# Two chained transformer models: the modulation panels on TensorE in four column groups instead of partly on GpSimd

## The chip, the cores and the metric

One core of one Trainium2 chip. The metric is the time of one execution on the device in microseconds (us); the kernel before has a median of 2692.15 us over three runs (2691.78, 2692.15, 2695.29). Less is better. TensorE multiplies, VectorE and ScalarE do elementwise work and read TensorE's results from the eight PSUM banks, GpSimd does elementwise work in SBUF, and SyncE issues the loads of the weights.

## The reference, cut to what matters

Two models in a row, each of two layers, on 256 tokens of width 1024. The first has a mixing part (layer 0: block attention "moba" and a pooling; layer 1: a gated MLP and a gated delta rule), a cross attention and a convolution FFN in each layer. The second is modulated by a vector c:

```python
def adaln(x, g, shift, scale):
    return rmsnorm_2(x, g) * (1 + scale[:, None, :]) + shift[:, None, :]

for l in range(DEPTH):                       # 2 layers
    mod = jax.nn.silu(c) @ ada_w[l] + ada_b[l]          # c is [1, 1024], ada_w[l] is [1024, 6144]
    sh_m, sc_m, g_m, sh_f, sc_f, g_f = jnp.split(mod, 6, axis=-1)
    hn = adaln(x, mix_norm_g[l], sh_m, sc_m)
    ...                                      # hn @ w_in[l]; four attentions; y = concat @ w_out[l]
    x = x + g_m[:, None, :] * y
    hn = adaln(x, ffn_norm_g[l], sh_f, sc_f)
    ...                                      # f = swiglu (layer 0), top-2-of-8 experts (layer 1)
    x = x + g_f[:, None, :] * f
```

One of the four attentions, the indexed one, scores all keys by `relu(q_idx . k_idx)` in eight heads of 32, weights and sums the heads, and keeps the best 64 keys of each query. Another, the differential one, is normalised per head behind the attention.

## The kernel before, in words

All weights reach SBUF as panels of 1 MB (128 partitions x 2048 floats), issued by SyncE in one fixed order into a ring of six slots. `load_one` waits, before it issues panel n, until panel n-6 is released (`released`), so a panel is issued when the product that reads the one six places ahead is done. 48 of the 583 panels hold the modulation weights `ada_w`: 2 layers x 6 parts x 4 quarters of 256 columns, in the order of `ADA_ORDER`. Parts 2 and 5 are the gates (rows, kept in GATE); the others are shift and scale (columns, kept in MODC).

Before the change, the panels go two ways. 17 are multiplied on TensorE by `ada` (L1071): a stationary COND of 128x128 (silu(c), spread over 128 columns), 256 moving columns, eight products for each panel, into the banks from 4 on. `ADA_AT` gives the places: one panel each at xat0, ffn0, mix1, xat1 and ffn1, four at mix2, three at ffn2, three at mix3 and two at ffn3. `transpose_norm` (L623) calls `ada` first and then waits for the normalised rows (`xhat_ready`), so that these products stand in the time in which the norm is computed. VectorE reads them out in `ada` (L2325 to L2334).

The other 31 panels are lent to GpSimd (`lend` L557, `LENT_AHEAD`): `sum_lent` (L2717) multiplies a panel with silu(c) in four pieces (L2731), adds (L2734, L2736) and leaves 128 x 256 partial sums in one of three buffers LENTS (L2737). `take` (L565) joins the partitions on TensorE with a product against ones (L573 for gates, L576 for columns), and VectorE reads that in `taken`. GpSimd holds two panels in the mixing of layer 0, ten in the cross attention xat0, eleven in mix1 and eight in xat1.

The stages follow one another as mix0 (moba), xat0, ffn0, mix1 (with the levels of a triangular inverse and the delta rule), xat1, ffn1, mix2, ffn2, mix3, ffn3 (experts). Each has a norm before it: ScalarE squares and sums the rows of H (L1474), VectorE makes the factor and XH (L1954), TensorE transposes XH (L632), ScalarE and VectorE read the transposes out with gain or modulation. At the entries of the FFNs ScalarE has first to split the first halves of the first gate and up panels into a high and a low part (`first_halves` L1423, the copy is at L1457); then it squares. VectorE does the low part (L2124). In the FFN TensorE's up products are L885, the down products L899.

The moba attention (`paired_attention` L651) goes over eight units in pairs: scores (L677), softmax on ScalarE and VectorE (scaling by the reciprocal: L2008), transposes (L664), mixing with the values (L693, outputs in two column groups of 64). Panels of the next stages are multiplied beside the units (`BESIDE`). The pooling product L1106 and the projection (`project`, L838) follow; each projection reads four panels. In mix2 and mix3 TensorE scores the index heads with `index_scores` (L1285), tile by tile; ScalarE evacuates them (L1873); VectorE sums them (`index_sum`, L2633 and L2635); the panels c_qi, c_ki, b_qd, b_kvd, a_q, a_k, a_v come between. The squares of the differential output, DSQ, are made on ScalarE in `keep` (L1584), amid the attention of the last groups, and summed on TensorE behind it by `diff_sums` (L758).

A name of a bank is claimed by TensorE (`claim`; `claim_aside` takes one of two banks in turn), filled, read out by another engine, and then free again. All engines work through their own stream in order.

## Time and profile before

| | |
|---|---|
| median of three runs | 2692.15 us |
| the profiled execution, its time | 2694.97 us |
| its span (first to last instruction) | 2693.2 us |
| mean granted clock of TensorE | 0.982 |
| busy: TensorE, VectorE, ScalarE, GpSimd | 2578.2 us (96%), 1726.7 (64%), 1306.3 (49%), 301.1 (11%) |
| `ada` on TensorE (L1083) | 272 records, 60.2 us busy |
| GpSimd's products (L2731) | 124, 130.8 us busy |
| panels in SyncE's queue, ada_w | 48, 4.8 us from issue to landing (median) |

The profile is read for what TensorE waits for: it is busy for 96% of the span, and the chain of work that ended last runs almost wholly through it. The busy shares of the other engines are an average over stages that differ much: the experts fill the second half of the span, while the modulation panels all lie in the first 1645 us. A product of floats (f32) stands as two records in the trace. The duration of a group of records ends with a modelled tail, so prices of products are taken from start to start. "granted clock" 1.0 is 2.4 GHz and 0.50 is 1.2 GHz.

### The profile page before, as it was taken

Reading aid. Unit: us, or ns where it says so; the run is one execution under the profiler, and the core shown is the slowest. Engines: PE = TensorE matmul, PEld = TensorE weight load, DVE = VectorE, ACT = ScalarE, POOL = GpSimd, SP = SyncE. Lnnn points to the kernel's source line nnn. Section 1 sums busy time; section 2 is a strip of 40 time slices with the busy share of each in tenths; the row PEclk is TensorE's granted clock in tenths of the full one; section 3 lists DMA queues with packets and bytes.
Section 4 is the critical chain, followed back from the end, with each engine's and each line's share of the span. In section 5 each row is a group of like instructions: output and inputs, shape, how many; then the busy total and the mean of one; then the engine's idle time right before and its main releaser. Section 6 shows DMA issues by size and latency. Waiting matters only on the chain.

```text
span 2693.2 us, 39037 instructions
## 1 busy us (share of the span) xinstructions
PE 2578.2 (96%) x13620; PEld 2139.9 (79%) x13620; DVE 1726.7 (64%) x2535; ACT 1306.3 (49%) x1931; POOL 301.1 (11%) x288
## 2 busy tenths in 40 slices
PE   7899999999899999989999988999999999999998
PEld 7677899887487998767998766888888888887886
DVE  1312777663225773465553464989898988889897
ACT  2211544421123442243331243777777777777775
POOL 0465000870270000000000000000000000000000
PEclk9999999999899999999999998999999999999999
DMA  8345544442355444315444313989898989899897
GB/s 321 125 179 213 208 185 168 177 174 92 110 219 198 190 183 179 110 48 195 183 183 174 107 58 135 377 320 383 325 379 323 370 329 378 335 346 355 341 355 285
DMA packets 87635, 627.29 MB, mean 233 GB/s; under 512 B 9760, under 2 KB 9920, under 8 KB 12800
## 3 DMA queue, kind: packets, MB, share of 16 engines
q1 hardware_dynamic: 84512, 613.45, 60.1%
...
HBM read 625.06 MB, written 1.05 MB: 232 GB/s over the span
## 4 chain that ended last, share of the span: by engine, by line
PE 92%; DVE 4%; ACT 2%; issue 1%; POOL 1%; DMA 0%; DVEq 0%; SPq 0%; ACTq 0%; POOLq 0%
PE bank L994 23%; PE bank L885 14%; PE bank L1022 11%; PE bank L605 11%; PE bank L899 7%; PE bank L618 6%; PE bank L838 6%; PE bank L1122 1%; PE bank L1083 1%; PE bank L964 1%; PE bank L1037 1%; PE bank L1009 1%; PE bank L677 1%; PE bank L693 1%; PE bank L664 1%
## 5 line engine op out<-in xcount | busy, mean ns | idle before, releaser
L1457 ACT ACTIVATE sb_parts<-sb_ring 128x1024 fp32r<-128x1024 f32 x873 | 872.9, 1053 | 125.4 <-PE bank L1022 38.9
L2222 DVE TENSOR_TENSOR sb_parts<-sb_ring,sb_parts 128x1024 fp32r<-128x1024 f32 x675 | 786.4, 1217 | 10.8 <-ACT sb_parts L1457 10.8
L994 PE MATMUL bank<-sb_parts 128*128 128x512 f32 x2688 | 661.4, 396 | 2.5 <-DVE sb_parts L2214 1.8
L994 PEld LDWEIGHTS bank<-sb_parts 128*128 128x128 f32 x2688 | 495.0, 188 | 113.3 <-issue 9.4
L885 PE MATMUL bank<-sb_parts 128*128 128x256 f32 x3168 | 387.1, 284 | 7.1 <-DVE sb_XT L2147 5.8
L885 PEld LDWEIGHTS bank<-sb_parts 128*128 128x128 f32 x3168 | 385.9, 193 | 9.9 <-issue 7.7
L1022 PE MATMUL bank<-sb_parts 128*128 128x512 f32 x1344 | 323.9, 390 | 0.0
L1022 PEld LDWEIGHTS bank<-sb_parts 128*128 128x128 f32 x1344 | 251.7, 188 | 52.1
L1457 ACT ACTIVATE sb_REG<-bank 128x512 f32<-128x512 f32 (+2 forms) x119 | 67.9, 576 | 408.3 <-PE bank L605 211.4
L605 PE MATMUL bank<-sb_XT,sb_ring 128*128 128x256 f32 x1152 | 257.5, 384 | 6.9 <-DVE sb_XT L1969 3.9
L2124 DVE TENSOR_TENSOR sb_parts<-sb_ring,sb_parts 128x1024 fp32r<-128x1024 f32 x198 | 232.8, 1219 | 34.3 <-ACT sb_parts L1457 34.3
L605 PEld LDWEIGHTS bank<-sb_XT,sb_ring 128*128 128x128 f32 x1152 | 219.5, 192 | 40.4 <-issue 10.9
L899 PE MATMUL bank<-sb_parts 128*128 128x512 f32 x792 | 185.3, 390 | 0.0
L838 PE MATMUL bank<-sb_ring,sb_OT 128*128 128x512 f32 x384 | 169.8, 603 | 3.3 <-DVE sb_OT L2033 1.7
L899 PEld LDWEIGHTS bank<-sb_parts 128*128 128x128 f32 x792 | 146.6, 188 | 29.4 <-DVE sb_parts L2124 0.2
L2731 POOL TENSOR_TENSOR sb_ring<-sb_ring,sb_small 128x512 f32<-128x512 f32 x124 | 130.8, 1085 | 197.5 <-DVE sb_XH L1954 165.4
L838 PEld LDWEIGHTS bank<-sb_ring,sb_OT 128*128 128x128 f32 x384 | 73.6, 193 | 94.6 <-issue 91.5
L618 PE MATMUL bank<-sb_ring,sb_XT 128*128 128x256 f32 (+1 forms) x512 | 117.5, 391 | 5.8 <-ACT sb_O L1873 4.2
L618 PEld LDWEIGHTS bank<-sb_ring,sb_XT 128*128 128x128 f32 x512 | 99.1, 202 | 22.6 <-issue 9.2
L1457 ACT ACTIVATE sb_parts<-bank 128x256 fp32r<-128x256 f32 (+1 forms) x130 | 52.7, 413 | 122.0 <-PE bank L1009 112.2
L1474 ACT ACTIVATE sb_XH<-sb_H 128x1024 f32<-128x1024 f32 x24 | 25.2, 1049 | 161.9 <-DVE sb_H L2097 102.0
L2236 DVE TENSOR_TENSOR sb_parts<-bank,sb_parts 128x256 fp32r<-128x256 f32 x112 | 47.3, 422 | 76.1 <-ACT sb_parts L1457 76.1
...
## 6 DMA issues: line engine op xcount, KB each, us to landing
sb_ring<-in_moe_panels SPq DMA_DIRECT2D x342, 1024.0 KB, 5.0
sb_ring<-in_ada_w SPq DMA_DIRECT2D x48, 1024.0 KB, 4.8
sb_ring<-in_ffn_w_up SPq DMA_DIRECT2D x44, 1024.0 KB, 4.9
sb_ring<-in_ffn_w SPq DMA_DIRECT2D x33, 1024.0 KB, 4.8
sb_ring<-in_w_in SPq DMA_DIRECT2D x26, 1024.0 KB, 4.8
sb_ring<-in_ffn_w_down SPq DMA_DIRECT2D x22, 1024.0 KB, 7.1
sb_ring<-in_xattn_wkv SPq DMA_DIRECT2D x16, 1024.0 KB, 6.9
sb_ring<-in_od_w_in SPq DMA_DIRECT2D x12, 1024.0 KB, 5.6
```

What stands on the lines that cost most here:

```text
L605: m = nc.tensor.matmul(ps[:, c * T:c * T + T], wt[:, k, c * P:c * P + P], rhs[:, k, :], start=k == 0, stop=k == KD - 1)
L618: m = nc.tensor.matmul(ps[:, tb * T:tb * T + w], lhs[:, k, tb * P:tb * P + P], wt[:, k, 0:w], start=k == 0, stop=k == KD - 1)
L838: m = nc.tensor.matmul(acc[j][:, :], OT[:, 2 * pair + c, j // 2 * P:j // 2 * P + P], wt[:, c, j % 2 * 512:j % 2 * 512 + 512], start=kk == ...
L885: m = nc.tensor.matmul(banks[b][:, half * T:half * T + T], w[:, kk, :], x[:, kk, :], start=t == 0, stop=t == len(terms) - 1)
L899: m = nc.tensor.matmul(banks[4 + j][:, :], h[:, g, tb], w[u][:, half], start=start and c == 0 and t == 0, stop=stop and c == 1 and t == 2, ...
L994: m = nc.tensor.matmul(banks[par][:, :], x[:, k, :], w[:, cols], start=k == 0 and t == 0, stop=k == KD - 1 and t == 2, skip_group_check=True)
L1022: m = nc.tensor.matmul(banks[4 + j][:, :], h[:, par, c, :], w[:, cols], start=start and c == 0 and t == 0, stop=stop and c == 1 and t == 2 ...
L1457: return nc.scalar.activation(out, in_, ACT.Copy)
L2124: V_.tensor_tensor(as_panel(LOW[u], what), half_panel(n, what, c, it), as_panel(HIGH[u], what), ALU.subtract).then_inc(sem("low_ready"), 1)
L2222: V_.tensor_tensor(LOW[u], ring[slot][:, 1024 * c:1024 * c + 1024], HIGH[u], ALU.subtract) \
L2236: V_.tensor_tensor(HTL[:, par, :, :], banks[6 + par][:, 0:T].rearrange("p (c t) -> p c t", c=2), HTH[:, par, :, :], ALU.subtract).then_inc ...
L2731: m = G.tensor_tensor(w[:, k:k + 2, :], w[:, k:k + 2, :], c[:, k:k + 2, :], ALU.mult)
```

## The change

- `lend`, `sum_lent`, LENTS, COND, SPREAD and `ADA_AT` go; GpSimd has no part in the modulation.
- The 48 panels form 24 pairs; `ADA_PAIRS` gives two pairs (four panels) to each of twelve places: in moba before the mixing of the last but one pair of units, at xat0, ffn0, mix1, in the levels 2 and 3 of mix1 (one pair each), behind the scan of the delta rule, at xat1, ffn1, mix2, ffn2, mix3, ffn3.
- `ada` takes a stationary operand of 32 columns (silu(c) of one k, broadcast) and puts the product k into the output partitions 32 (k mod 4) and on: eight products for a panel as before, k = 0 to 3 into four column groups and k = 4 to 7 added to them. Two panels share a bank of 512 columns.
- ScalarE copies the bank (128x512) into one of four buffers PARTIAL (`partials`): after the read-out of the norm in most places, in the FFNs before the walk over the chunks.
- `take(i)` joins the pair's partial sums against ones, on TensorE; VectorE scales by 1/32 and adds the bias or the row. The takes of pairs 0 to 3 stand in xat0, 4 to 7 behind the qkv panels of mix1, 8 and 9 in levels 4 and 5, 10 to 13 in xat1, 14 to 17 in mix2, 18 to 21 in mix3, 22 and 23 in the experts. Pairs 4, 5, 10, 11, 16, 17, 22 and 23 are gates.
- `index_scores` claims two banks and emits the products of its two tiles in turn.
- The squares DSQ move from `keep` to behind the whole attention.
- In moba the panel p1 is multiplied beside unit 2 instead of unit 1.

The diff, cut: left out are the old `ada` (L1071, removed), the calls of `index_scores` (now with a pair of tiles), the removed calls of `lend`, the calls of `take` and `taken` that only change their argument, VectorE's `ada` and GpSimd's `sum_lent`, both removed whole.

```diff
@@ -153,9 +153,7 @@
         ROW = sb("ROW", ROW_W)
         REG_W = 13900
         small = sb("small", 544)
-        COND = sb("COND", KD, P)
-        LENTS = sb("LENTS", 3, T)
-        SPREAD = sb("SPREAD", 2, P)
+        PARTIAL = sb("PARTIAL", 4, 2 * T)
         ROUNDS = sb("rounds", 1, dt=mybir.dt.int32)
         small_index = sb("small_index", NT, 8, dt=U32)
         MODC = sb("MODC", 2, 48)
...
@@ -492,26 +490,14 @@
 
 
         ADA_ORDER = [("ada", l, part, q) for l in range(2) for part in range(6) for q in range(4)]
-        ADA_AT = {"xat0": 1, "ffn0": 1, "mix1": 1, "xat1": 1, "ffn1": 1, "mix2": 4,
-                  "ffn2": 3, "mix3": 3, "ffn3": 2}
-
-
-        LENT_AHEAD = {"mix0": (("out", "mix0", 0), ("out", "mix0", 2)),
-                      "xat0": tuple(("xq", 0, j) for j in range(4)) + (("xk", 0, 0), ("xk", 0, 1)) + tuple(("xv", 0, j) for j in range(4)),
-                      "mix1": tuple(("qkv", j) for j in range(6)) + (("u", 0), ("u", 1), ("vz", 0), ("vz", 1), ("gate", 0)),
-                      "xat1": tuple(("xq", 1, j) for j in range(4)) + tuple(("xv", 1, j) for j in range(4))}
-
-
-        TAKE_LATER = {"xat0": {("xq", 1): (2, 4), ("xq", 3): (1, 5), ("xk", 0): (1, 6), ("xk", 1): (1, 7),
-                               0: (1, 7), 1: (1, 6), 2: (1, 7), 3: (1, 6), 4: (1, 7), 5: (1, 6), 6: (1, 7)},
-                      "xat1": {("xq", 2): (1, 4), ("xq", 3): (1, 5), 0: (1, 7), 1: (1, 6), 2: (1, 7), 3: (1, 6),
-                               5: (1, 7), 6: (1, 6)}}
-        LENT_TO = {name: stage for stage, names in LENT_AHEAD.items() for name in names}
-        lent, taken_by = [], {}
+        ADA_PAIRS = {h: (2 * i, 2 * i + 1) for i, h in enumerate(
+            ("moba", "xat0", "ffn0", "mix1", "levels", "delta", "xat1", "ffn1", "mix2", "ffn2", "mix3", "ffn3"))}
+        TAKE_AFTER = {"xat0": {("xq", 1): 0, ("xq", 3): 1, ("xk", 0): 2, ("xk", 1): 3},
+                      "xat1": {("xq", 0): 10, ("xq", 1): 11, ("xq", 2): 12, ("xq", 3): 13}}
         EARLY_KEYS = 4
 
 
-        BESIDE = {"moba": {0: ("p", 0), 1: ("p", 1), 4: ("xk", 0, 2), 6: ("xk", 0, 3)},
+        BESIDE = {"moba": {0: ("p", 0), 2: ("p", 1), 4: ("xk", 0, 2), 6: ("xk", 0, 3)},
                   "x0": {j: ("xv", 0, j) for j in range(4)},
                   "x1": {j: ("xv", 1, j) for j in range(4)}}
         LATE = {0: "d_q", 1: "d_k", 3: "d_v", 4: "c_q", 5: "c_k", 6: "c_v"}
@@ -519,7 +505,7 @@
         SELECT_AT = {0: (0, 0, 4), 1: (0, 4, 8), 3: (1, 0, 4), 4: (1, 4, 8)}
         BIAS_AT = 6
         KEYS_FIRST = {0: (0, 1), 1: ()}
-        ada_done, ada_hooks, ada_panels = [0], {}, {}
+        ada_panels = {}
 
 
         GAINS = {"mem": ("mem_norm", 0), "mix0": ("norm_mix", 0), "mix1": ("norm_mix", 8), "xat0": ("norm_xattn", 0),
...
@@ -554,28 +540,40 @@
                     b, n = turns[name]
                     pe.wait_ge(drained[b], n)
 
-            def lend(stage):
-
-                lent.append((state["panel"], ADA_ORDER[ada_done[0]], stage))
-                ada_panels[state["panel"]] = ADA_ORDER[ada_done[0]]
-                ada_done[0] += 1
-                released[state["panel"]] = (sem("panel_summed"), len(lent))
-                state["panel"] += 1
-
-            def take(hook, n, bank=None):
-
-                first = sum(len(x) for x in taken_by.values())
-                taken_by[hook] = list(range(first, first + n))
-                ps = claim_aside(("taken", hook)) if bank is None else claim(("taken", hook), bank)
-                for x, i in enumerate(taken_by[hook]):
-                    pe.wait_ge(sem("panel_summed"), i + 1)
-                    if lent[i][1][2] in (2, 5):
-                        m = nc.tensor.matmul(ps[:, x * T:x * T + T], cst("ones"), LENTS[:, i % 3, :], start=True, stop=True)
+            def ada(hook, in_banks=(4, 5)):
+
+                pe.wait_ge(sem("silu_cond"), 1)
+                for x, i in enumerate(ADA_PAIRS[hook] if isinstance(hook, str) else hook):
+                    ps = claim(("ada", i), in_banks[x]) if in_banks else claim_aside(("ada", i))
+                    used = []
+                    for half in range(2):
+                        ada_panels[state["panel"]] = ADA_ORDER[2 * i + half]
+                        pn, slot = panel()
+                        used.append(pn)
+                        wt = cols_of(slot)
+                        for k in range(KD):
+                            g = 32 * (k % 4)
+                            m = nc.tensor.matmul(ps[g:g + 32, half * T:half * T + T],
+                                                 sm("cond", 8)[:, k:k + 1].broadcast_to([P, 32]), wt[:, k, :],
+                                                 start=k < 4, stop=k >= 4, skip_group_check=True)
+                    filled(m, ("ada", i))
+                    for pn in used:
+                        release(pn, ("ada", i))
+
+            def take(i):
+
+                ps = claim_aside(("taken", i))
+                wait_read(("ada", i))
+                for x in range(2):
+                    if ADA_ORDER[2 * i + x][2] in (2, 5):
+                        m = nc.tensor.matmul(ps[:, x * T:x * T + T], cst("ones"), PARTIAL[:, i % 4, x * T:x * T + T],
+                                             start=True, stop=True)
                     else:
                         for c in range(2):
-                            m = nc.tensor.matmul(ps[:, x * T + c:x * T + c + 1], LENTS[:, i % 3, c * P:c * P + P],
+                            m = nc.tensor.matmul(ps[:, x * T + c:x * T + c + 1],
+                                                 PARTIAL[:, i % 4, x * T + c * P:x * T + c * P + P],
                                                  cst("ones")[:, 0:1], start=True, stop=True)
-                filled(m, ("taken", hook))
+                filled(m, ("taken", i))
 
             def panel():
 
...
@@ -622,7 +616,8 @@
 
             def transpose_norm(n):
 
-                ada(n, ADA_AT.get(n, 0))
+                if n in ADA_PAIRS:
+                    ada(n)
                 pe.wait_ge(sem("xhat_ready"), 2 * (TURNED.index(n) + 1))
                 for j in range(4):
                     ps = claim(("norm", n, j))
...
@@ -680,6 +675,8 @@
                                     filled(m, ("scores", key, s))
                         for s in two:
                             beside_units(key, s)
+                    if key == "moba" and q == len(us) // 2:
+                        ada("moba", (6, 7))
                     if q >= 2:
                         wait_read(*[("turned", key, t) for t in ended])
                         name = ("mixed", key, us[ended[0]]["group"])
...
@@ -1201,8 +1175,10 @@
                     panel_tok(("gate", lv - 2))
                 else:
                     panel_T(("xk", 1, lv - 4), rhs=MT)
-                if lv > 1:
-                    take(("mix1", lv + 2), 1)
+                if lv in (2, 3):
+                    ada((lv + 6,), None)
+                elif lv > 3:
+                    take(lv + 4)
                 pe.wait_ge(sem("level_ready"), lv)
                 for tb in range(NT):
                     products(("y", lv), M_of(gM), M_of(gX), tb)
...
@@ -1262,6 +1238,7 @@
                     m = nc.tensor.matmul(ps[rows, h * P:h * P + P], gQK[rows, 4 * tb + h, rows], gVN[rows, h, :],
                                          start=n == 0, stop=True)
                 filled(m, ("so", n))
+            ada("delta")
             pe.wait_ge(sem("delta_out"), 1)
             turn_outputs("mix1", list(range(4, 8)))
             wait_read(("sgu", 0), ("sgu", 1))
...
@@ -1278,13 +1255,16 @@
                 normed(n)
                 k2 = f"s{layer}"
 
-                def index_scores(tb, j):
-                    ps = claim((k2, "idx", tb, j))
+                def index_scores(tb, js):
+
+                    tiles = [claim((k2, "idx", tb, j)) for j in js]
                     for c in range(2):
-                        b = 32 * j
-                        m = nc.tensor.matmul(ps[:, c * T:c * T + T], QI[b:b + 32, c, tb * P:tb * P + P],
-                                             KI4[b:b + 32, :], start=True, stop=True)
-                    filled(m, (k2, "idx", tb, j))
+                        for ps, j in zip(tiles, js):
+                            b = 32 * j
+                            m = nc.tensor.matmul(ps[:, c * T:c * T + T], QI[b:b + 32, c, tb * P:tb * P + P],
+                                                 KI4[b:b + 32, :], start=True, stop=True)
+                            if c == 1:
+                                filled(m, (k2, "idx", tb, j))
 
                 panel_T((k2, "c_qi"))
                 pn, slot = panel()
...
@@ -1476,6 +1456,14 @@
                 act.wait_ge(sem("mean_square_ready"), idx + 1)
                 nc.scalar.activation(sm("sd", 2), sm("ms", 2), ACT.Sqrt).then_inc(sem("deviation_ready"), 1)
 
+            def partials(hook):
+
+                for i in ADA_PAIRS[hook] if isinstance(hook, str) else hook:
+                    wait_full(act, ("ada", i))
+                    if i >= 4:
+                        wait_full(act, ("taken", i - 4))
+                    read_out(copy(PARTIAL[:, i % 4, :], bank_of(("ada", i))[:, :]), ("ada", i))
+
             def root_table():
 
                 act.wait_ge(sem("const_loaded"), 16)
@@ -1499,6 +1487,8 @@
                                                      bias=MODC[:, l, at + k:at + k + 1],
                                                      scale=MODC[:, l, at + 8 + k:at + 8 + k + 1])
                     read_out(m, ("norm", n, j))
+                if n in ADA_PAIRS:
+                    partials(n)
 
             def exponentials(key, s):
 
@@ -1536,6 +1526,8 @@
                 paired = key[0] != "x"
                 for s in range(len(us) + TURN_LAG):
                     if paired:
+                        if key == "moba" and s == len(us):
+                            partials("moba")
                         beside_units(key, s)
                         if s >= TURN_LAG:
                             turned(key, s - TURN_LAG)
...
@@ -1579,9 +1571,6 @@
                 dst = OT[:, u["chunks"], cols]
                 m = copy(dst, bank_of(name)[:, :].rearrange("p (c t) -> p c t", c=n))
                 read_out(m, name)
-                if u["turns"] == 2:
-                    wait_drained(act, name)
-                    nc.scalar.activation(DSQ, dst, ACT.Square).then_inc(sem("diff_squares"), 1)
 
             def outputs(name, chunks):
                 for j in range(0, len(chunks) // 2, 2):
...
@@ -1626,6 +1615,7 @@
                                                      bias=MODC[:, l, at + k:at + k + 1],
                                                      scale=MODC[:, l, at + 8 + k:at + 8 + k + 1])
                     m.then_inc(sem("input_high"), 1)
+                partials(n)
 
                 def chunk(it, c, i):
                     b = 2 * (it % 2) + c
...
@@ -1898,6 +1891,8 @@
                 act.wait_ge(sem("lambda_sums"), layer + 1)
                 nc.scalar.activation(sm("lexp", 2), sm("lsum", 2), ACT.Exp).then_inc(sem("lambda_exp"), 1)
                 attention(k2)
+                wait_drained(act, ("mixed", k2, 0))
+                nc.scalar.activation(DSQ, OT[:, 0:2, :], ACT.Square).then_inc(sem("diff_squares"), 1)
                 act.wait_ge(sem("diff_mean"), layer + 1)
                 nc.scalar.activation(sm("dsd", 8), sm("dms", 8), ACT.Sqrt).then_inc(sem("diff_deviation"), 1)
                 n = f"ffn{2 + layer}"
...
-            def taken(hook):
...
+            def taken(i):
+
+                name = ("taken", i)
                 wait_full(dve, name)
...
-                        m = V_.tensor_tensor(dst, ps, dst, ALU.add)
+                        m = V_.scalar_tensor_tensor(dst, ps, 1.0 / 32, dst, ALU.mult, ALU.add)
...
+                taken(14 + 4 * layer)
+                taken(15 + 4 * layer)
                 index_sum(0)
...
+                taken(16 + 4 * layer)
+                taken(17 + 4 * layer)
                 index_sum(1)
```

## Rows read from the trace of the kernel before

**Rows 1.** The page, part 4, then the cores view: the chain by engine; span, clock.

```profile
PE 92%; DVE 4%; ACT 2%; issue 1%; POOL 1%; DMA 0%; DVEq 0%; SPq 0%; ACTq 0%; POOLq 0%
...
core 0: 2693.2 us, clock 0.982
```

**Rows 2.** TensorE's timeline, 75 to 110 us: start, duration, engine, line, operation [idle before, releaser].

```profile
79.09 0.63 PE L664 MATMUL bank<-sb_CST,sb_REG 128*128 128x128 f32 x4 [1.73 <-DVE sb_REG L2008]
...
101.99 1.09 PE L693 MATMUL bank<-sb_REG 128*64 128x128 f32 x16 [1.80 <-ACT sb_REG L1457]
...
106.41 1.00 PE L664 MATMUL bank<-sb_CST,sb_REG 128*128 128x128 f32 x4 [1.52 <-DVE sb_REG L2008]
```

**Rows 3.** VectorE's timeline beside it, and all instructions of line 2008 (min/median/max ns).

```profile
101.60 2.52 DVE L2008 TENSOR_SCALAR sb_REG<-sb_REG,sb_small 128x256 f32<-128x256 f32 x2
...
L2008 DVE TENSOR_SCALAR sb_REG<-sb_REG,sb_small x112: 344/353/1423, 72.1 to 1599.1; 128x256 f32<-128x256 f32 x112
```

**Rows 4.** TensorE's timeline: four modulation panels; a product in two column groups, one in none.

```profile
98.08 1.10 PE L693 MATMUL bank<-sb_REG 128*64 128x128 f32 x16
99.10 1.09 PE L664 MATMUL bank<-sb_CST,sb_REG 128*128 128x128 f32 x8
...
1025.14 13.98 PE L1083 MATMUL bank<-sb_ring,sb_COND 128*128 128x256 f32 x64
```

**Rows 5.** TensorE's timeline: the take of two panels, and what follows it.

```profile
163.36 0.95 PE L576 MATMUL bank<-sb_CST,sb_LENTS 128*128 128x1 f32 x8
164.17 1.11 PE L605 MATMUL bank<-sb_XT,sb_ring 128*128 128x256 f32 x4
```

**Rows 6.** Windows, TensorE alone: stretch, us, busy (instructions), granted clock, DMA share, GB/s.

```profile
106.50:113.30 6.80, 6.02 (x28) 0.50 0.01 2
684.60:693.60 9.00, 8.16 (x16) 0.50 0.01 2
1243.20:1250.00 6.80, 4.18 (x20) 0.50 0.02 4
```

**Rows 7.** Timeline of all engines at the entry of the first FFN.

```profile
274.86 0.33 SPq L2812 DMA_DIRECT2D sb_ring<-in_ffn_w_down  x1
...
275.59 1.06 ACT L1474 ACTIVATE sb_XH<-sb_H 128x1024 f32<-128x1024 f32 x1 [15.52 <-DVE sb_H L2097]
...
279.92 1.97 PE L632 MATMUL bank<-sb_CST,sb_XH 128*128 128x128 f32 x16 [1.64 <-DVE sb_XH L1954]
```

**Rows 8.** TensorE's timeline: waits in the first cross attention.

```profile
180.50 5.84 PE L605 MATMUL bank<-sb_MT,sb_ring 128*128 128x256 f32 x18 [1.93 <-DMA sb_ring<-in_xattn_wkv]
...
240.63 0.63 PE L726 MATMUL bank<-sb_CST,sb_REG 128*128 128x128 f32 x4 [0.87 <-DVE sb_REG L2008]
...
246.25 0.58 PE L576 MATMUL bank<-sb_CST,sb_LENTS 128*128 128x1 f32 x4 [0.98 <-POOL sb_LENTS L2737]
```

**Rows 9.** The page, part 6: issues of FFN panels, KB each, median us to landing.

```profile
sb_ring<-in_ffn_w_up SPq DMA_DIRECT2D x44, 1024.0 KB, 4.9
```

**Rows 10.** Timeline of all engines at the entries of mix2 and ffn2.

```profile
1034.37 1.42 DVE L1954 TENSOR_SCALAR sb_XH<-sb_H,sb_small 128x1024 f32<-128x1024 f32 x2
...
1227.70 10.52 PE L1083 MATMUL bank<-sb_ring,sb_COND 128*128 128x256 f32 x48
...
1230.95 1.06 ACT L1474 ACTIVATE sb_XH<-sb_H 128x1024 f32<-128x1024 f32 x1 [5.96 <-DVE sb_H L2104]
...
1238.06 1.91 PE L632 MATMUL bank<-sb_CST,sb_XH 128*128 128x128 f32 x16
...
1245.82 10.46 PE L885 MATMUL bank<-sb_parts 128*128 128x256 f32 x70 [5.84 <-DVE sb_XT L2147]
```

**Rows 11.** TensorE's timeline at the end of the delta rule.

```profile
684.61 1.97 PE L816 MATMUL bank<-sb_CST,sb_O 128*128 128x128 f32 x8 [7.49 <-DVE sb_O L2595]
```

**Rows 12.** TensorE's timeline in mix2, the product behind the index scores.

```profile
1092.70 2.64 PE L618 MATMUL bank<-sb_ring,sb_XT 128*128 128x256 f32 x6 [2.08 <-ACT sb_O L1873]
```

**Rows 13.** All instructions of line 1584 on ScalarE (min/median/max ns).

```profile
L1584 ACT ACTIVATE sb_XH<-sb_OT x2: 630/630/631, 1176.0 to 1581.8; 128x512 f32<-128x512 f32 x2
```

146 lines of the change are left out of this document (34 added, 112 removed).

## The prediction

> **What bounds the kernel now.** The chain that ended last is read first: TensorE holds 92% of it [rows 1]. So an edit counts by what it adds to or takes from TensorE's own stream, and by the waits inside it; the timelines of TensorE show those. VectorE, ScalarE, GpSimd and the panels matter only where TensorE waits for them. The long loops (conv FFNs, SwiGLU, experts) are not touched. What follows is the front part, where the attention ends, the norms and the takes lie.
>
> In the moba attention the reader is to see TensorE's waits at 79.09, 101.99 and 106.41 [rows 2], and beside them VectorE's scaling of two halves in 2.52 us where the median of one is 353 ns [rows 3]. GpSimd was multiplying and adding at that moment; I take it that the two get in each other's way.
>
> **Prices.** A modulation panel is 8 products, 16 records; four panels start 13.81 us before the next work (64 records of 216 ns), 3.45 us each [rows 4]. The new form puts 32 columns of stationary operand into each of four column groups. The nearest row is the two-group product of the attention: 16 records in the time in which 8 of full width go [rows 4], that is, two groups run side by side. No row shows four. Bounds: 3.45 us a panel if the groups take turns, 0.86 if all four run together. I take 0.87, as two groups did reach the full factor, so a hook (four panels) costs 3.6 us with the changes of tile shape.
>
> The Trainium skill, "TensorE: Matmul & The Clock Gate", Part 3, gives a factor of 2.38 for three column groups and 3.07 for four row groups, less than the full four. By that a panel would be 1.13 us and a hook 4.5; it would add about 1 us at each of the two hooks that nothing covers. The rows show two groups at the full factor, so they neither bear that out nor exclude it.
>
> A take of two column panels is 8 records, 0.81 us from 163.36 to 164.17 [rows 5]; of two gate panels 4 records of 216 ns, 0.86. Before, the 31 panels of GpSimd were taken; now all 48 are.
>
> **Part by part, in us against the profiled execution.**
>
> *Moba.* Without GpSimd the two slow scalings cost about 0.7 each, so the last turning can start 3.2 earlier than 106.41; p1, read out a unit later, frees VectorE at 79.09 (1.5). The new hook (3.6) goes into the idle time ahead of 101.99 and costs about 1.3 beyond it. Waits: -3.4. From 106.5 to 113.3 TensorE had half of its clock, with 6.02 busy [rows 6], 3.0 lost and 2.6 of it on the path; with its idle time filled by products I expect full clock: -2.6. Together **-6.0** (bounds -9 and 0).
>
> *Norm before xat0.* As at ffn0, where the same work stands, the transposes start 5.1 after the projection's end (274.86 to 279.92 [rows 7]), and the old panel fills 3.45 of that. The hook's 3.6 fits in: 0.
>
> *xat0.* Twelve panels were taken there, two together (0.81), six columns at 0.36 and four gates at 0.43: 4.69. Four pairs of columns are 3.24: -1.45. The wait of 1.93 for a wkv panel, the 0.87 behind a slowed scaling and the 0.98 behind GpSimd's last sum [rows 8] go, with 0.27 behind the last: the ring no longer holds ten lent panels until GpSimd has summed them. **-5.5**, bounds -6.5 and -1.5.
>
> *FFN entries (ffn0, ffn1).* Ahead of the transposes at 279.92 stands VectorE's normalisation and ahead of it ScalarE's squares at 275.59 [rows 7]. ScalarE first splits the first gate and up panels (`first_halves`), and only then squares. A panel may be issued when the one six places ahead is released. The projection's four panels are r0 to r3; with one modulation panel behind them the first up panel is r6 and waits for r0. With four it is r9 and waits for r3, the last of the projection, at 274.86, where the row of SP shows such a release [rows 7]. A panel lands 4.9 later [rows 9], so 279.7; the copy takes 1.05, squares at 280.7, transposes 4.33 later at 285.0 instead of 279.92: **+5.1** each, +10.2. Bounds 0 and +6 each. The modulation products that lie here are covered by it.
>
> *Clock at these entries.* TensorE then has 6.7 us without work behind the 3.6 of the hook. At ffn2 it waited 5.84 for VectorE before its first up product, with the clock at 0.50 from 1243.2 to 1250.0 and 4.18 busy in those 6.8 [rows 6, 10]. I put +2.5 on each, half of a stretch of some 5 us: **+5.0**, bounds 0 and 3.4 each.
>
> *Norms of mix1 and xat1.* As at xat0: the stall is 5.1 and takes 3.6; 0. The takes of xat1 come out 0.2 less.
>
> *mix1 stage.* Takes: seven columns and four gates singly, 4.24, become four column and two gate pairs, 4.96 (+0.7); the hooks in levels 2 and 3, two panels each, lie in TensorE's stream with nothing to fill: +3.9 with four changes of shape; a VectorE undisturbed by GpSimd gives 0.8 back, an estimate: **+3.8**.
>
> *Delta.* The hook lies in TensorE's wait of 7.49 for the normalisation of the outputs [rows 11]: 0. That wait ran on into a stretch at 0.50, 684.6 to 693.6, with 8.16 busy [rows 6], 4.1 lost. With the wait half filled I expect **-3.0**, bounds -4.1 and 0.
>
> *mix2 entry.* 13.81 of products lay beside the norm, which ended at 1035.8 (1034.37 + 1.42 [rows 10]); they ended at 1038.95 [rows 4]. With 3.6 the norm sets the start: **-3.1**; clock, as TensorE then idles 7: **+2.4** (0 to 3.4).
>
> *mix2 stage.* Four pairs are taken here, two of columns and two of gates: +3.4. VectorE adds four gate rows of 128x256 just ahead of its index sum, each a little over the 353 ns of a scaling of that size [rows 3], and TensorE waits 2.08 at 1092.70 for ScalarE, which waits for that sum [rows 12]: +1.7. The square DSQ (0.63 [rows 13]) is moved from amid the attention to behind it, ahead of the sums of the differential part: its 0.63, a drain and the wake of TensorE make +1.5, an estimate. **+6.6**, bounds +3.4 and +8. Index scores in turn: both orders put products of different row groups next to each other: 0.
>
> *ffn2.* The squares started at 1230.95, the transposes at 1238.06 behind three old panels, which began at 1227.70, at the projection's end [rows 10]. Now the first up panel is issued there and lands at 1232.6, 1.7 behind the squares' old start, and the transposes come at about the same time: 0; clock **+1.75**.
>
> *mix3.* 10.4 of products go, its norm ends 2.8 sooner: **-2.8**, clock **+1.0**. Its stage: takes +3.2, VectorE +0.6 (column pairs are short adds), DSQ +1.5: **+5.3**. *ffn3:* 0, clock **+0.7**.
>
> ScalarE's new copies of 128x512 (24 of 0.59) lie beside TensorE's work. GpSimd's whole work goes, and but for the waits above TensorE waited for none of it; GpSimd's own loads that stood behind its sums wait for projections and go out at the same time or sooner. SP moves the same 48 panels among the same others; what changes is their place, and outside the FFN entries they are loaded ahead (bounds 0 and +1 at each of the four other norms).
>
> **Sum.** Without the clock: -3.4 -5.5 +10.2 +3.8 -0.2 -3.1 +6.6 -2.8 +5.3 = +10.9. Clock: -2.6 -3.0 +5.0 +2.4 +1.75 +1.0 +0.7 = +5.25. Together **+16.2**. The profiled execution took 2694.97, 2.8 over the median of 2692.15; against the median it gives **2708 us**.
>
> **Rivals.**
> *Two groups at a time.* The two-group row is all that is shown; a hook is then 6.9. Moba and mix1's stage pay 3.4 each, three norms 1.8 each, about 4 of the clock's price comes back: 2716. Chance 0.08.
> *The groups take turns, so the change doesn't do what it says.* 13.8 a hook: 10.2 more in moba and in the levels, 8.7 at three norms, 3 to 7 at the other six: +79 less 5 of clock, some 2780. Against it speaks the two-group row. 0.04.
> *No wait for the up panel.* If the ring runs otherwise than I read it, or the squares do not stand behind the split, 10.2 and 5.0 go: 2693, no change. For it: no row shows the changed order. Against: at ffn2 the squares stood behind VectorE's sum, so the order on ScalarE costs nothing there and can't be seen. 0.15.
> *Faster: the clock.* The place is TensorE before and behind the norms. If the products in the gaps keep the clock up, the 10.85 that I add for new idle time at six entries (2.5, 2.5, 2.4, 1.75, 1.0, 0.7) falls away: +5.35. If beside that the old stretches at 0.50 shorten too (the mean clock of 0.982 [rows 1] leaves 48 of 2693 us missing; delta 1.1 more, ffn2's 2.1, the rest elsewhere), a third of the 48, some 17, more: -11.7, 2680. It decides from 10.7 us beyond the first 10.85. For it: hooks in the gaps of moba and delta. Against: 684.6 to 693.6 at 0.50 behind a gap of 7.49 [rows 6, 11]. 0.11.
> The Trainium skill, same page, "Why this matters for your kernels", advises against idle gaps of TensorE between bursts, after which the clock goes back; that speaks against this change, which shortens what fills mix2, ffn2, mix3 and ffn3. With the gaps of 5.84 and 7.49 the trace agrees.
>
> **How the numbers follow.** The forecast itself has 0.62, with its own range 2698 to 2722. A measurement of this kernel can tell about 0.2%, 5.4 us, from no change. Slower: 0.60 + 0.08 + 0.04 + 0.01 = 0.73; same: 0.02 + 0.12 = 0.14; faster: 0.11 + 0.02 = 0.13. The range 2688 to 2728 holds forecast, two at a time and no wait, and leaves out the clock, the turns and the tails.
>
> **What would show each step.** One hook takes 3.5 to 3.7 us at full clock and the records of four groups start together (7: two at a time; 14: turns). ScalarE's squares at ffn0 and ffn1 stand behind a DMA of up, 5 us after the last product. Transposes of mix2 start about 10.7 behind the last down product, and TensorE's clock shows 0.5 behind them. Scalings in moba take 0.35 each. The wait for ScalarE before a_v is nearly 4. The forecast is wrong if the entries of ffn0 and ffn1 are as before, or if the clock in section 2 of the page has more nines in the front half than now.

## The result, and the profile after

The changed kernel takes 2710.84 us (median of five runs, 2706.67 to 2714.17) against 2692.15 for the kernel before: a ratio of 1.0061 with a 95% interval of 1.0051 to 1.0072, slower by 0.6%. The forecast was 2708, its range 2688 to 2728. The profiled execution has a span of 2710.2 us, 17.0 over that of the kernel before; the forecast for this comparison was +16.2.

First the page of the changed kernel (busy shares, chain by engine). They answer to [rows 1].

```profile
PE 2581.6 (95%) x14174; PEld 2132.4 (79%) x14174; DVE 1683.2 (62%) x2510; ACT 1318.5 (49%) x1955; POOL 26.4 (1%) x40
...
PE 92%; DVE 3%; ACT 2%; issue 1%; DMA 1%; DVEq 0%; SPq 0%; ACTq 0%
```

GpSimd went from 301 us to 26, and TensorE is still as good as the whole chain. Its busy time is 3.4 us more, its share 1% less: it waits more. The list of TensorE's waits says for whom; the columns are who waited, for what, us in total, times, longest. First the kernel before, then the changed one.

```profile
PE bank L632 <- DVE sb_XH L1954: 19.8, 7, 11.1
PE bank L664 <- DVE sb_REG L2008: 10.4, 15, 1.7
```

```profile
PE bank L627 <- DVE sb_XH L1949: 49.9, 10, 10.8
PE bank L659 <- DVE sb_REG L2001: 6.0, 12, 0.8
...
PE bank L753 <- ACT sb_XH L1895: 2.4, 2, 1.2
```

The transposes of the norms (L632, now L627) waited 19.8 us in total and now wait 49.9; the scalings of the attention (L2008, now L2001) cost 10.4 and now 6.0; and the sums of DSQ (L753) wait for ScalarE, which they did not before. The three lines are the trade in short. The 30 us more of waiting at L627 are not all loss: at mix2, ffn2, mix3 and ffn3 they stand where longer modulation products stood before.

**The new products** (answer to [rows 4]), on TensorE's timeline of the changed kernel:

```profile
100.86 3.66 PE L556 MATMUL bank<-sb_ring,sb_small 128*32 128x256 f32 x64
104.45 0.77 PE L690 MATMUL bank<-sb_REG 128*64 128x128 f32 x10
...
585.87 1.93 PE L556 MATMUL bank<-sb_ring,sb_small 128*32 128x256 f32 x32
587.74 2.05 PE L1099 MATMUL bank<-sb_REG 128*128 128x128 f32 x16
```

Four panels, 64 records, start 3.59 us before the next work (100.86 to 104.45), where 13.81 was the price of the old form: all four column groups run side by side, a factor of 3.85 with the changes of shape in it. The Trainium skill, "TensorE: Matmul & The Clock Gate", Part 3, has 2.38 for three column groups and 3.07 for four row groups, and no figure for four column groups. The 3.85 measured here decides against carrying one of these lower factors over to this case. A pair of panels takes 1.87 (585.87 to 587.74). The two take forms and the index scores (L1285 before, L1264 now: 1.14 and 1.13 for eight records) cost what they did.

**Stage by stage.** The starts of the modulation products mark the end of a projection or an FFN, the starts of the transposes (L632, now L627) the end of a norm. From these marks in both traces:

| stretch | before, us | after, us | difference | forecast |
|---|---|---|---|---|
| start to end of mix0 | 140.98 | 137.81 | -3.2 | -6.0 |
| norm of xat0 | 5.25 | 5.16 | -0.1 | 0 |
| xat0 | 128.44 | 119.90 | -8.5 | -5.5 |
| norm of ffn0 | 5.25 | 10.43 | +5.2 | +5.1 |
| ffn0 | 189.58 | 190.24 | +0.7 | +2.5 |
| norm of mix1 | 5.26 | 5.16 | -0.1 | 0 |
| mix1 to the end of the delta rule | 209.85 | 215.56 | +5.7 | +3.8 |
| projection of mix1 | 33.41 | 33.26 | -0.2 | -3.0 |
| norm of xat1, xat1 | 112.26 | 111.00 | -1.3 | -0.2 |
| norm of ffn1 | 5.26 | 10.26 | +5.0 | +5.1 |
| ffn1 | 189.60 | 190.69 | +1.1 | +2.5 |
| norm of mix2 | 13.82 | 10.61 | -3.2 | -3.1 |
| mix2 | 188.74 | 198.62 | +9.9 | +9.0 |
| norm of ffn2 | 10.36 | 10.13 | -0.2 | 0 |
| ffn2 | 196.43 | 197.69 | +1.3 | +1.75 |
| norm of mix3 | 10.36 | 7.56 | -2.8 | -2.8 |
| mix3 | 188.55 | 194.78 | +6.2 | +6.3 |
| norm of ffn3 | 7.58 | 7.49 | -0.1 | 0 |
| experts to the end | 1052.2 | 1053.8 | +1.6 | +0.7 |

(The clock's terms of the forecast stand with the stage behind the norm; mix2 is 6.6 and 2.4, mix3 5.3 and 1.0.)

**The entry of ffn0** (answers to [rows 7]), timeline of all engines of the changed kernel:

```profile
262.97 2.70 SPq L2747 DMA_DIRECT2D sb_ring<-in_ffn_w_up  x3
...
266.96 0.44 SPq L2747 DMA_DIRECT2D sb_ring<-in_ffn_w_up  x1
268.01 1.06 ACT L1437 ACTIVATE sb_parts<-sb_ring 128x1024 fp32r<-128x1024 f32 x1 [6.03 <-DMA sb_ring<-in_ffn_w_up]
268.98 1.04 ACT L1454 ACTIVATE sb_XH<-sb_H 128x1024 f32<-128x1024 f32 x1
...
273.30 3.43 PE L627 MATMUL bank<-sb_CST,sb_XH 128*128 128x128 f32 x16 [6.77 <-DVE sb_XH L1949]
```

Line by line: the modulation products start at 262.87, SyncE issues up panels from 262.97 on, ScalarE's split (the copy of `first_halves`) of one waits 6.03 us for the transfer until 268.01, its squares start right behind at 268.98, and the transposes at 273.30, after TensorE waited 6.77. The prediction had the wait, its place and its length.

**The clock** (answers to [rows 6]), windows of the changed kernel behind ffn0's, ffn1's and mix2's norms, and the projection of mix1:

```profile
269.50:276.30 6.80, 3.00 (x14) 0.50 1.02 422
684.26:717.52 33.26, 32.43 (x72) 0.87 0.45 172
836.10:842.90 6.80, 4.12 (x20) 0.50 1.02 397
1037.50:1044.30 6.80, 3.67 (x16) 0.50 0.99 389
```

Three stretches of 6.8 us at 0.50, new, with 3.00, 4.12 and 3.67 us busy in them; at most half of each is lost. Before the change no stretch at 0.50 lies within 14 us behind these norms. The projection of mix1 has a mean of 0.87, as before the change.

**mix2** (answers to [rows 12] and, for the squares, [rows 13]): reads of takes on VectorE, and TensorE's waits before a_v and before the sums of DSQ.

```profile
1097.19 1.41 DVE L2314 SCALAR_TENSOR_TENSOR sb_GATE<-bank,sb_GATE 128x256 f32<-128x256 f32 x4
...
1100.16 3.33 PE L612 MATMUL bank<-sb_ring,sb_XT 128*128 128x256 f32 x7 [3.40 <-ACT sb_O L1866]
...
1205.56 1.95 PE L753 MATMUL bank<-sb_CST,sb_XH 128*128 128x1 f32 x16 [1.21 <-ACT sb_XH L1895]
```

The four gate rows take 1.41; the wait before a_v grew from 2.08 to 3.40; the sums wait 1.21 for the square. Windows over the whole of mix2, TensorE alone, the kernel before and then the changed one:

```profile
1038.96:1227.70 188.74, 174.37 (x923) 0.96 0.30 106
1040.08:1238.70 198.62, 182.46 (x946) 0.94 0.29 100
```

Of the 9.9 us more, 1.8 are idle time (16.2 against 14.4) and 8.1 busy time. The takes account for 3.4 of the busy time. TensorE is at 0.50 for 24.7 us of this stage, 13.7 before, and was busy there for almost all of it (22.9 and 13.6): half of the difference is 4.7, the rest.

**Moba** (answers to [rows 3]), VectorE's timeline of the changed kernel:

```profile
102.34 0.62 DVE L2001 TENSOR_SCALAR sb_REG<-sb_REG,sb_small 128x256 f32<-128x256 f32 x2
...
103.80 0.62 DVE L2001 TENSOR_SCALAR sb_REG<-sb_REG,sb_small 128x256 f32<-128x256 f32 x2
```

The pair of scalings that took 2.52 takes 0.62.

### The profile page after: what moved, and what is told of

Same layout as the page of the kernel before. It is cut to its first block, busy times and chain, and to the rows that moved or that the text cites. A ratio compares the mean times of both kernels' runs of the same rounds, so it can differ in the third digit from the quotient of the medians.

```text
span 2710.2 us, 39877 instructions
## 1 busy us (share of the span) xinstructions
PE 2581.6 (95%) x14174; PEld 2132.4 (79%) x14174; DVE 1683.2 (62%) x2510; ACT 1318.5 (49%) x1955; POOL 26.4 (1%) x40
## 4 chain that ended last, share of the span: by engine, by line
PE 92%; DVE 3%; ACT 2%; issue 1%; DMA 1%; DVEq 0%; SPq 0%; ACTq 0%
PE bank L989 23%; PE bank L878 14%; PE bank L601 12%; PE bank L1017 11%; PE bank L892 6%; PE bank L831 6%; PE bank L612 6%; PE bank L1099 2%; PE bank L1032 1%; PE bank L959 1%; PE bank L627 1%; ACT sb_XH L1454 1%; PE bank L1004 1%; PE bank L672 1%; PE bank L690 1%
## 5 line engine op out<-in xcount | busy, mean ns | idle before, releaser
L1926 DVE COPY sb_REG<-bank 128x512 f32<-128x512 f32 x21 | 14.5, 691 | 133.6 <-PE bank L601 78.8
L2152 DVE SCALAR_TENSOR_TENSOR sb_REG<-bank,sb_COL,sb_REG 128x255 f32<-128x255 f32 x88 | 42.4, 482 | 74.5 <-ACT sb_REG L1438 68.3
```

## The experiments

All are the changed kernel with one edit, unless said otherwise. The kernel before was run beside them: its median was 2691.98 us beside the first kernel of experiment 1 and experiments 3 and 4, 2695.29 beside the second kernel of experiment 1 and experiments 2, 5 and 6, and 2694.52 beside experiment 7, against 2692.15 beside the changed kernel. So differences of totals across experiments are uncertain by some 3 us, and those of single runs by more; where it can be done, stages of the profiles are compared, by the marks of the table.

**1. Where the FFN entries' wait comes from.** Two kernels.

```diff
-            first_halves("ffn0", high_split("ffn0"))
+            first_halves("ffn0", high_split("ffn0"), ("gate",))
             norm("ffn0")
+            first_halves("ffn0", high_split("ffn0"), ("up",))
```

and the same at ffn1; in VectorE's `norm` the low part of the up panel goes behind the normalisation.

> The changed kernel (median 2710.84 us), but at the entries of ffn0 and ffn1 ScalarE splits only the first gate panel before the norm, and the first up panel behind the squares and the root; VectorE's low part of the up panel goes behind its normalisation. If the squares wait there for the up panel (my theory), the transposes at both entries come about 5 us after the end of the projection instead of 10.4, less 0.3 for ScalarE's split of the up panel ahead of its read-outs, and the clock stretches behind them (269.5 and 836.1) vanish or shorten: 2701 us, -9 to -11. Rival: the entries are longer because of the four modulation panels or their transfers; then nothing moves, 2711.

Measured: 2703.38 us (2702.13 to 2704.69), ratio to the kernel before 1.0046 (1.0029 to 1.0063): 7.5 us less than the changed kernel, not 10. By the profile the two entries are 3.3 and 3.1 us shorter (7.17 and 7.10). The entry of ffn0, on the timeline:

```profile
258.44 1.06 ACT L1437 ACTIVATE sb_parts<-sb_ring 128x1024 fp32r<-128x1024 f32 x1 [23.35 <-DMA sb_ring<-in_ffn_w_up]
...
259.53 1.23 DVE L2117 TENSOR_TENSOR sb_parts<-sb_ring,sb_parts 128x1024 fp32r<-128x1024 f32 x1 [33.59 <-ACT sb_parts L1437]
...
260.67 2.48 DVE L2092 TENSOR_TENSOR sb_H<-bank,sb_H 128x512 f32<-128x512 f32 x4
263.18 1.06 ACT L1454 ACTIVATE sb_XH<-sb_H 128x1024 f32<-128x1024 f32 x1 [3.69 <-DVE sb_H L2092]
...
267.51 3.68 PE L627 MATMUL bank<-sb_CST,sb_XH 128*128 128x128 f32 x16 [3.51 <-DVE sb_XH L1951]
```

The wait for the up panel is gone, but the transposes stand 7.2 us behind the projection's end, not 5.2: the gate panel, one place ahead, lands late as well (ScalarE's split at 258.44), VectorE makes its low part until 260.7 and only then adds the four sums (260.67), so that the squares start at 263.18. The stretch at 0.50 behind the norm is gone at ffn1 and still there at ffn0 (266.4 to 273.2). The second kernel puts both splits behind the norm, on both engines:

```diff
-                first_halves(f"ffn{layer}", low_split(f"ffn{layer}"), ("gate",))
                 add_sum(n)
...
-            first_halves("ffn0", high_split("ffn0"))
             norm("ffn0")
+            first_halves("ffn0", high_split("ffn0"))
```

> As e1_norm_first, but at ffn0 and ffn1 the splits of the first gate panel go behind the norm as well, on ScalarE and on VectorE. In e1 the entries are 7.1 us from the end of the projection to the transposes, not the 5.2 of the kernel before; there VectorE's low part of the gate panel (landed at 258.44, two panels before the up panel) stands ahead of its four additions of the sums. If that is the rest of the wait, the entries are 5.2 us here, 5.2 less than in the changed kernel; VectorE's two low parts (2.4 us) then stand ahead of its half of the input and may give 1 us back at each: 2700 us (2697 to 2704 with the scatter of a single run). Rival: the rest is something else, and the entries stay at 7.1.

Measured: 2699.49 us (one run).

```profile
261.83 1.06 ACT L1454 ACTIVATE sb_XH<-sb_H 128x1024 f32<-128x1024 f32 x1 [26.09 <-DVE sb_H L2090]
...
266.16 1.97 PE L627 MATMUL bank<-sb_CST,sb_XH 128*128 128x128 f32 x16 [1.51 <-DVE sb_XH L1949]
```

The products start at 260.99 and the transposes at 266.16, 5.17 behind, at ffn1 5.16. That is all of the 5.2 and 5.0 lost at the two norms: it was the order of the splits before the norm, together with panels that come late because three more stand ahead of them in the ring. No rival that blames the products themselves is left, as they are the same here. The stretch at 0.50 behind ffn0's norm is gone in this profile, yet ffn0 takes 190.23 (190.24 in the changed kernel): it looks as if the splits behind the norm cost about what the clock gave; no run separates the two.

**2. The clock's price at the entries.**

```diff
                     used = []
+                    if x == 0:
+                        for _ in range({"ffn0": 14, "ffn1": 14, "mix2": 15, "ffn2": 14, "mix3": 8, "ffn3": 8}.get(hook, 0)):
+                            nc.tensor.matmul(ps[:, 0:T], ident, cst("chunked")[:, 0:T], start=True, stop=True)
```

> The changed kernel with products of constants (128x128 by 128x256, results overwritten) ahead of the modulation products at six entries: 14 each at ffn0, ffn1 and ffn2, 15 at mix2, 8 each at mix3 and ffn3, so that TensorE is busy until about 0.5 us before the transposes. They add work only in time in which it waits. If the clock falls because TensorE idles there, the stretches at 0.50 that begin at 269.5, 836.1, 1037.5, 1245.7 and 1453.9 vanish and the long one at 1655.3 shortens; the prediction priced these six at 10.85 together, the trace of the change at about 1.5 to 2.5 each: 2702 us, -6 to -11. Rival: the stretches come from what follows (the gaps and short transposes behind the norm), so the fill changes nothing or less than 2: 2710.

Measured: 2701.54 us (ten runs, 2699.34 to 2704.14), ratio to the kernel before 1.0025 (1.0015 to 1.0035), 9.3 us less than the changed kernel, with more work in it. TensorE's timeline and two windows:

```profile
262.29 6.21 PE L551 MATMUL bank<-sb_CST 128*128 128x256 f32 x28
268.43 3.66 PE L559 MATMUL bank<-sb_ring,sb_small 128*32 128x256 f32 x64
272.69 1.97 PE L630 MATMUL bank<-sb_CST,sb_XH 128*128 128x128 f32 x16 [0.61 <-DVE sb_XH L1952]
...
262.29:276.00 13.71, 12.48 (x115) 1.00 0.51 197
1025.30:1044.00 18.70, 16.72 (x132) 1.00 0.48 189
```

The norm takes as long as ever (10.40 from the first product to the transposes), TensorE is busy in it, and the clock stays at 1.00 in both windows. The stretches behind the norms of ffn0, ffn1, mix2 and mix3 are gone; at ffn2 one of two is left (1248.3 to 1255.2), and at the experts 6.8 of 17.1 us (from 1654.5). Over the six stages behind the filled norms the trace shows -0.6 (ffn0), -1.1 (ffn1), -0.6 (mix2), -1.7 (ffn2), -1.3 (mix3) and -3.4 (experts) against the changed kernel: 8.7 us, where the prediction had 10.85. (The experts, with the same code there, took 1051.9 and 1055.8 in two other profiles, so that term is the least certain.) At ffn0 and ffn1 less is won than the half of 3.00 and 4.12; probably ScalarE and VectorE, which take over the transposes there, set the pace, but no run shows that. The Trainium skill, "TensorE: Matmul & The Clock Gate", "Why this matters for your kernels", advises against idle gaps of TensorE between bursts, after which the clock goes back. This run agrees: with the gaps filled the two windows have 1.00, where the changed kernel has stretches at 0.50.

**3. What the column groups are worth.** Two kernels: neighbours in the same group, and no groups.

```diff
-                        for k in range(KD):
+                        for k in (0, 4, 1, 5, 2, 6, 3, 7):
                             g = 32 * (k % 4)
```

> The changed kernel with the eight products of a modulation panel in the order k = 0, 4, 1, 5, 2, 6, 3, 7, so that two products of the same column group stand behind each other. If groups run side by side only when neighbours in the stream lie in different groups and products start in order, each pair of the same group takes turns: two at a time at best, a hook 6 to 7 us instead of 3.5. The hooks in moba and in the levels lengthen by about 3 each and three norms by 1.7: about 2721 us. Rival: the array sorts the groups itself whatever the order: 3.5 us a hook and 2711.

```diff
-                            m = nc.tensor.matmul(ps[g:g + 32, half * T:half * T + T],
-                                                 sm("cond", 8)[:, k:k + 1].broadcast_to([P, 32]), wt[:, k, :],
-                                                 start=k < 4, stop=k >= 4, skip_group_check=True)
+                            m = nc.tensor.matmul(ps[:, half * T:half * T + T],
+                                                 sm("cond", 8)[:, k:k + 1].broadcast_to([P, P]), wt[:, k, :],
+                                                 start=k == 0, stop=k == KD - 1)
```

with 1/128 in the read-outs.

> The changed kernel, but each modulation product has its stationary operand spread over 128 columns (silu(c) broadcast, summed over k in all partitions) and the read-out scales by 1/128 instead of 1/32; places, panels and takes as in the change. This is the price of 48 panels on TensorE without column groups. By my prediction's rival: 13.8 us a hook, about +79 and a little of the clock back: 2785 us (2775 to 2795). Rival: most hooks lie under other waits, so that less than half of it shows: 2745 or less.

Measured: 2707.44 and 2773.51 us (one run each). The first, on TensorE's timeline and in the window of mix1's projection:

```profile
100.34 3.73 PE L556 MATMUL bank<-sb_ring,sb_small 128*32 128x256 f32 x64
104.00 0.88 PE L690 MATMUL bank<-sb_REG 128*64 128x128 f32 x12
...
683.26:714.33 31.07, 30.24 (x73) 0.95 0.49 185
```

Four panels take 3.66 (100.34 to 104.00): my theory for this run fell, and its rival holds. The groups go on side by side with two products of the same group behind each other in the stream. The second:

```profile
100.54 13.98 PE L555 MATMUL bank<-sb_ring,sb_small 128*128 128x256 f32 x64
114.44 1.09 PE L689 MATMUL bank<-sb_REG 128*64 128x128 f32 x16
...
core 0: 2771.7 us, clock 0.989
```

Four panels take 13.90 without groups, 10.3 more, 124 in twelve hooks; the span is 61.5 over that of the changed kernel, less than the 74 of the prediction's rival and of what was expected here. By stages, 9.9 come in mix0, 52.3 in the nine norms (each is now 13.81 long, set by the products) and 12.2 in mix1, 74.4 together; so about 50 of the 124 lay in waits. The other stages, whose products are the same, are 12.9 shorter, and the mean clock is 0.989 here and 0.978 in the changed kernel: with the norms filled the clock gives back more than the 5 that were allowed for.

**4. The squares DSQ.**

```diff
                 read_out(m, name)
+                if u["turns"] == 2:
+                    wait_drained(act, name)
+                    nc.scalar.activation(DSQ, dst, ACT.Square).then_inc(sem("diff_squares"), 1)
...
-                wait_drained(act, ("mixed", k2, 0))
-                nc.scalar.activation(DSQ, OT[:, 0:2, :], ACT.Square).then_inc(sem("diff_squares"), 1)
```

> The changed kernel with the squares DSQ made again on ScalarE amid the attention, as before the change. My theory: 1.5 us in mix2 and in mix3 each, visible as TensorE's wait before the sums of the differential part: 2708 us, and those two stages 1.5 shorter each. Rival: the square has cover behind the attention, nothing moves.

Measured: 2700.76 us (one run). Only the stages count here, and against the first run of experiment 3, whose mix1 took as long (245.0 and 245.1): mix2 from its norm on 194.55 us against 197.59, mix3 191.78 against 194.82, so 3.0 each, twice the forecast. 1.2 of it is the wait of the sums; in the other run a stretch at 0.50 of 6.8 us follows at 1200.2 and one of 3.4 at 1613.2, in this kernel 3.4 at 1199.8 and none in mix3. The other profiles bear that out: all eight with the squares behind the attention have 3.4 or 6.8 us at 0.50 there in mix2 and in mix3, the three with the squares amid it at most 3.4 in mix2 and none in mix3. So the wait is followed by time at half clock that it would not have without it.

**5. The reads of the takes.**

```diff
-                taken(16 + 4 * layer)
-                taken(17 + 4 * layer)
                 index_sum(1)
+                taken(16 + 4 * layer)
+                taken(17 + 4 * layer)
```

> The changed kernel, but in mix2 and mix3 VectorE reads takes 16 and 17 (20 and 21) out behind its second index sum instead of ahead of it. My theory: the four gate rows there (1.41 us) hold the index sum, ScalarE and TensorE before a_v; its wait goes from 3.40 back to about 2.1 in mix2 and by 0.5 in mix3, and the stretch at 0.50 that follows may shorten: -2 to -4 us, 2708. Rival: the bank that the take holds is then needed earlier than it is read, and TensorE waits for it instead: 2711 or more.

Measured: 2708.23 us (one run). TensorE's waits of this kernel:

```profile
PE bank L612 <- ACT sb_O L1866: 4.2, 2, 2.1
```

Two waits of 2.1, where the changed kernel had 3.40 and 2.34; no wait for the bank came in their place. The size of the wait in mix2 (1.3) is measured. The stages are shorter by less: mix2 198.30 instead of 198.62, as a stretch at 0.50 behind it is longer (6.8 us, 3.4 in the changed kernel), and mix3 194.31 instead of 194.78. The difference of the totals is within what single runs scatter.

**6. GpSimd against VectorE.** GpSimd does 30 products of 128x512 on two PARTIAL buffers, not used yet at that time, from the end of its pooling on (left out here: the memset before them and ScalarE's wait for their end):

```diff
+            for _ in range(30):
+                step(G.tensor_tensor(PARTIAL[:, 3, :], PARTIAL[:, 2, :], PARTIAL[:, 2, :], ALU.mult))
```

> The changed kernel with 30 products of 128x512 on GpSimd, on two of the PARTIAL buffers before they are used, from the end of its pooling (some 92 us) on, each waiting for the one before: GpSimd is busy as it was before the change, with nothing that depends on it but ScalarE's later copy. If GpSimd's work is what slows VectorE, VectorE's two scalings at the end of moba take 1.5 to 2.5 us again instead of 0.62, the last transposes of moba come 1 to 3 us later and the stage ends 1 to 4 us later. Rival: GpSimd's activity as such does nothing to VectorE (the slow scalings came from what it read or from the lent panels): 0.62 stays.

Measured: 2713.55 us (one run). Timelines of VectorE, GpSimd and TensorE:

```profile
102.33 1.73 DVE L2003 TENSOR_SCALAR sb_REG<-sb_REG,sb_small 128x256 f32<-128x256 f32 x2
...
104.17 2.13 DVE L2003 TENSOR_SCALAR sb_REG<-sb_REG,sb_small 128x256 f32<-128x256 f32 x2
...
92.79 33.50 POOL L2711 TENSOR_TENSOR sb_PARTIAL<-sb_PARTIAL 128x512 f32<-128x512 f32 x30
...
106.44 0.63 PE L659 MATMUL bank<-sb_CST,sb_REG 128*128 128x128 f32 x4 [0.32 <-DVE sb_REG L2003]
```

The scalings take 1.73 and 2.13 instead of 0.62 with nothing changed for VectorE but a busy GpSimd. TensorE however waits for them 0.32 only, and mix0 ends 0.45 later, not the 1 to 4 that I expected: the new products lie in the gap. In the changed kernel the slow VectorE would hardly be felt in moba; in the kernel before, TensorE waited 1.52 for it (106.41 [rows 2]).

**7. All together.** This kernel has both splits behind the norm (at ffn2 too), the squares amid the attention, the late reads, and the fill cut to the time that is left (3, 3, 15, 8, 8, 8 products).

> The changed kernel with what the runs point to put together: at ffn0, ffn1 and ffn2 both splits behind the norm (e9: -5.2 at two entries, 2.6 looked for at ffn2), the squares DSQ amid the attention (e4: about -3 in mix2 and in mix3), the reads of takes 16, 17, 20, 21 behind the index sum (e5: -1.3 and -0.3), and the fill of constants at six entries, shortened to three products at ffn0 and ffn1 and eight at ffn2, where less time is left (e6: -9 together, of which e9 already has the 5 of ffn0 and ffn1). Sum from 2710.84: -10.4 -2.6 -6 -1.6 -4.5 = 2686 us, 0.2 to 0.3% faster than the kernel before. Rival: the gains overlap, since each shortens the same stretches at half clock; then no better than 2692, level with the kernel before.

Measured: 2683.99 us (2683.51 to 2687.52, five runs), ratio to the kernel before 0.9964 (0.995 to 0.9978). It is 0.4% faster than the kernel before, and its median is 26.9 us under that of the changed kernel. The cores view of its profiled execution:

```profile
core 0: 2685.6 us, clock 0.985
```

The sum expected was 25.1 us; 26.9 came, and that is partly luck. Against the changed kernel's profile the entries of ffn0 and ffn1 give 10.2, where 10.4 was expected, but mix2 is 8.3 shorter, where experiments 2, 4 and 5 had shown 3.9 (it has 10.2 us at 0.50, not 24.7), mix3 2.9 instead of 4.8, and ffn2 with its norm 1.7 instead of 4.3: the norm ends 2.6 sooner, but TensorE then waits 7.54 for VectorE before the first up product, where it waited 4.59.

What wasn't settled or tried: the pairs in levels 2 and 3 of mix1 stand in TensorE's path (1.87 and 1.86 us each); no version that moves them to a norm with time left was run.

## Why the prediction was right, and where it was not

**The frame held.** The total and the sign were right, and of nineteen stretches ten are within 0.6 us of their forecast, eight of them norms. The price of a hook (3.6 forecast, 3.59 measured), the ring argument at the FFN entries (+5.1 each; +5.2 and +5.0), the norms of mix2 and mix3 (-3.1, -2.8; -3.2, -2.8) and the takes came out by their own working. Experiment 1 confirms the mechanism of the entries, the two kernels of experiment 3 the price of a hook and what sets the length of a norm. The takes were only read from the trace (0.81 for a pair of columns and 0.86 for a pair of gates at full clock; 0.88 and 0.96 between index scores). The rival without a wait for the up panel is excluded by experiment 1, the two of taking turns by the timeline, and the clock as a way to a faster kernel did not happen, though experiment 2 shows that it was worth 9 us.

**The ring argument was half of the cause at the entries.** The step that the first up panel is r9 and waits for r3 is right, but the gate panel one place ahead would have kept 2 us by itself (experiment 1), through VectorE's low part, which stands ahead of its sums, and not through ScalarE. The end was set by the up panel, so the number was right.

**Terms that were mis-sized.**
- *Start to end of mix0*, -6.0 forecast, -3.2 measured. 2.1 of the difference lies ahead of moba: the transposes of mem start at 43.65 before and at 45.73 after. In the changed kernel's execution TensorE's records there take 634 ns (median, 15.8 to 20.9 us from the start), in the other 379: the first rise of the clock came later. The clock rose 14.4 us after the start in the profile before, and 13.8 to 20.3 us after it in ten profiles of the changed kernel and its variants, with the same code there; the transposes of mem start at 43.23 in experiment 1's first profile. So it is no effect of the change. Moba itself is then -5.3.
- *xat0*, -8.5 instead of -5.5. The waits of 1.93, 0.87 and 0.98 went as forecast; two more went: 0.45 of the wait for VectorE's read-out of a take at 197.91 (0.86, now 0.41), and the stretch at half clock that followed the wait for the DMA, at 181.6, which cost 1.7; with them the terms make 7.7, and some 0.9 stay open. The prediction left a clock term out at a wait that it removed.
- *Delta*, -0.2 instead of -3.0. The hook filled half of the gap (3.90 left of 7.49), but the clock was at 0.50 from 682.5 to 692.8 all the same. In experiment 3's first profile, with the same places and waits there, the stage took 31.07, not 33.26, with a mean of 0.95: -2.3. Over nine profiles of the changed kernel and its variants it took 33.2 to 33.3 three times, 31.1 three times and 29.6 three times. The forecast is met in some executions and missed in others.
- *mix1*, +5.7 instead of +3.8: the pairs in the levels cost 3.7, the takes as forecast; the 0.8 that I gave back for VectorE was not found, and the stretches at 0.50 ahead of the wait at the delta rule's end are 10.2 us long, 6.8 before. Of eight other profiles with this stage unchanged (but for the order of the modulation products in one), four have 213.9 to 214.0 instead of 215.6, one 216.1, and three 219.5 to 219.6, with 13.7 us at 0.50 just ahead of that wait; those three are the ones in which the projection takes 29.6.
- *The clock at the six entries*, +10.85; 8.7 by experiment 2, but spread otherwise. At ffn0, ffn1 and mix2 it shows 0.6, 1.1 and 0.6 instead of 2.5, 2.5 and 2.4; at ffn2, mix3 and the experts 1.7, 1.3 and 3.4 instead of 1.75, 1.0 and 0.7. Half of the busy time at 0.50 was taken as the price, and at ffn0 and ffn1 it is an upper bound.
- *mix2*, +9.9 instead of +9.0, by errors that cancel. The waits grew by 1.8, not by 3.2 (1.7 and 1.5), and the clock cost 4.7 over the stage, not 2.4: the stretches at 0.50 inside the stage, which the prediction left as they were, grew (at a_v from 3.4 to 6.8 us), and one more came at the squares.
- *The squares*, +1.5; 3.0 each by experiment 4. The wait (1.2) was right, its effect on the clock left out. In part that was offset by the wait before a_v, which grew by 1.3 in mix2, not 1.7, and by 0.3 in mix3, not 0.6.
- *Experts*, +1.6 instead of +0.7. The takes of pairs 22 and 23 stand there, two gate pairs in TensorE's stream, which took 2.1 us together, in part at half clock (1671.69 to 1673.76). The prediction had forgotten them, and 2.1 us of idle time that went in this stage hide them: a missed step, small by luck.

The errors of xat0 (-3) and of delta, mix1 and the start (+2.8, +1.9, +2.1), the squares and the entries' clock have different signs, so the total of +16.2 is nearer to +17.0 than its parts deserve.
